# Cached attention on one core: key and value pages released and reloaded in runs of four, in place of whole batches

## The chip, the cores and the metric

The kernel runs on one core of one Trainium2 chip. The metric is device time in microseconds of one launch, lower is better. TensorE, VectorE (DVE), ScalarE (ACT), GpSimd (POOL) and SyncE (SP) each run a program of their own and meet through semaphores; SP and POOL also issue the DMAs.

## The reference, cut to what matters

One inference step of a two-layer decoder, for a prompt of 256 tokens and for 8 sample batches of 8 tokens each. The sample batches attend to a past of 2048 rows that lies in a paged cache: 16 pages of 128 rows for each batch, at places that a page table gives. Everything is float32.

```
past = cache_kv[page_table, :, c].reshape(Bd, past_len, N_KV, HEAD_DIM)   # c: 0,1 compressed  2 keys  3 values
...
idx = top_k(score, 16)                   # selected blocks of 64 rows, from the compressed branch's weights
s   = q . k * scale - slopes * dist      # over the selected blocks of the past
p   = masked_softmax(s)
o_s = p . v
o_w = window_dense(q, qpos, kw, vw)      # the same over the last 512 rows, from state_kv_win
o   = gates[0] * o_c + gates[1] * o_s + gates[2] * o_w
```

The change touches only how the key pages (c = 2), the value pages (c = 3) and the window rows of the sample batches come into SBUF, and when their buffers are free again. The feed-forward parts, the convolution, the prompt's attention and the compressed branch are as they were.

## The kernel before

The kernel is written engine by engine: `sp_program`, `pool_program`, `pe_program`, `act_program` and `dve_program`, each in its own order, with counting semaphores between them. The cached attention comes after the prompt's attention and ahead of the output projection `o`. It goes over the 8 batches b, NB = 8, with NPAGE = 16 pages each.

**Buffers.** There is one key buffer `kpg` and one value buffer `vpg`, 16 pages of 128 KB each (128 rows by 256 numbers). The window rows of a batch (keys and values, 1 MB) go into one of the two slots of `W`, slot u = b mod 2. `KTb` and `KTw` hold the transposed keys of one batch, `S` its scores, `PT` its transposed probabilities.

**SP (`load_keys`).** For each batch: `load_pages` waits (L318) until the key buffer is free (K_used, once for each batch), then issues 16 page DMAs (L322), each behind a register load of the page's number (L320); then it waits until the window slot is free (win_used) and issues the window DMA (L455). After the last batch's keys SP loads the last batch's values into the key buffer as well, and then goes on to the weights of `o` (L470).

**POOL.** For batches 0 to 6 the same `load_pages` fills the value buffer, once V_used has risen for a whole batch.

**TensorE (`batch_scores`, `batch_values`).** The order is scores(0), then scores(b+1) and values(b) for b from 0 to 6, then values(7). scores(b) turns the probabilities of batch b-1 (L881) between the other steps, waits for all 16 key pages (K_loaded), turns the keys in 8 groups of four 128x128 transposes (`turn_keys`, L901; four page groups of the first 128 columns, then four of the other 128), turns the window's keys in two more groups, and multiplies the queries with the turned keys in chunks of 512 (L895). K_used rises with the first transpose of the window's groups. The groups go through two PSUM banks, which ACT (L1291) and DVE (L1791) copy out in turn. values(b) waits for all 16 value pages (V_loaded), multiplies the probabilities with three short blocks, with the four window blocks (win_used rises with the last of them, which frees the slot for batch b+2), and with the 16 pages (all L942). V_used rises with the first transpose of the result (L957).

**ACT and DVE** work the masked softmax of batch b while TensorE works values(b-1). DVE also places the queries and chooses the blocks.

Of the kernel before, what the change touches and what calls it, by code (L numbers as in the profile page):

```python
# [14 lines left out]
P = 128  # L15
# [3 lines left out]
NB = 8  # L19
# [12 lines left out]
NPAGE = 16  # L32
PAST = NPAGE * PAGE
NPOOL = 160
# [23 lines left out]
S_SEL, S_NEW, S_WIN, S_WNEW, S_CMP = 0, PAST, PAST + TS, PAST + TS + WIN, PAST + 2 * TS + WIN  # L58
S_COLS = S_CMP + P
CREDIT = 2  # L60


def host_constants():
# [94 lines left out]
def program(nc, ins, outs, where):  # L158
    with ExitStack() as ctx:
# [9 lines left out]
        def sem(name):  # L169
            return ctx.enter_context(nc.semaphore(name))  # L170
# [30 lines left out]
        ptrow = sb("ptrow", 1, P, dt=I32)  # L201
# [63 lines left out]
        kpg, vpg = pages  # L265
# [6 lines left out]
        KTb = area(SF, 0, 2, PAST)  # L272
# [26 lines left out]
        slab_loaded = [sem("slab_loaded0"), sem("slab_loaded1")]  # L299
        gathered = [sem("gathered0"), sem("gathered1")]  # L300
        half_used = [sem("half_used0"), sem("half_used1")]
        K_loaded, V_loaded, K_used, V_used = map(sem, ("K_loaded", "V_loaded", "K_used", "V_used"))
        V_last_loaded = sem("V_last_loaded")
        win_loaded = [sem("win_loaded0"), sem("win_loaded1")]
        win_used = [sem("win_used0"), sem("win_used1")]

# [5 lines left out]

        cache = ins["cache_kv"]

        def load_pages(eng, b, c, page, used, count, loaded):

            eng.wait_ge(used, count)
            eng.sem_inc(m["passed"], 1)  # L318
            for k in range(NPAGE):
                n = eng.value_load(ptrow[0:1, bass.ds(b * NPAGE + k, 1)], min_val=0, max_val=NPOOL - 1)  # L320
                src = cache[bass.ds(n, 1), :, c, :, :].rearrange("a t g d -> t (a g d)")
                eng.dma_start(page[:, k, :], src).then_inc(loaded, 16)  # L322


        def sp_program(sp):
# [123 lines left out]
            def load_keys(i, off):  # L449

                b, u = i * 2 + off, off % 2
                load_pages(sp, b, 2, kpg, K_used, b + 1, K_loaded)
                sp.wait_ge(win_used[u], i + (off // 2 + 1))
                sp.sem_inc(m["passed"], 1)
                sp.dma_start(W[:, u, :], ins["state_kv_win"].rearrange("b (p r) c g d -> b p (r c g d)", r=WR)  # L455
                             [bass.ds(b, 1)].rearrange("a p c -> p (a c)")).then_inc(win_loaded[u], 16)

            load_keys(0, 0)
            with sp.Fori(0, NB // 2 - 1) as i:
# [1 line left out]
                    load_keys(i, u + 1)  # L461
            load_keys(NB // 2 - 1, 1)

            load_pages(sp, NB - 1, 3, kpg, K_used, NB + 1, V_last_loaded)
            wo = ins["w_o"][0].rearrange("(q g z d) n -> q g d z n", q=2, g=2, z=NZ)

            def out_proj(i, u):
# [11 lines left out]
        def pool_program(pool):  # L479
            pool.memset(eps[:, :], EPS).then_inc(m["pool_step"], 1)  # L480
            pool.memset(ones[:, :], 1.0).then_inc(m["pool_step"], 1)
            pool.memset(HF[:, 0:1], 0.0).then_inc(m["pool_step"], 1)
            pool.wait_ge(m["idx_ready"], 1)
            pool.wait_ge(m["evac_done"], OUTS_DOWN00 + CREDIT)
            pairs = cache.rearrange("n t (h c) g d -> (n t h) (c g d)", h=2)
            with pool.Fori(0, NB) as b:
                for u in range(2):
                    pool.wait_ge(half_used[u], b + 1)

                    pool.tensor_copy(cslot[:, 8 * u:8 * u + 8], cidx[:, bass.ds(b * CS + 8 * u, 8)]) \  # L490
                        .then_inc(m["slot_ready"], 1)
                    pool.wait_ge(m["slot_ready"], b * 2 + (u + 1))
                    pool.sem_inc(m["passed"], 1)
                    for s in range(8):
                        pool.indirect_dma_start(  # L495
                            out=STG[u][:, s, :], out_offset=None, in_=pairs,
                            in_offset=bass.IndirectOffsetOnAxis(ap=cslot[:, 8 * u + s:8 * u + s + 1], axis=0)) \
                            .then_inc(gathered[u], 16)

            pool.dma_start(outs[5].rearrange("b t c g d -> b (t c g d)")[:, 0:(WIN - NQ) * 512],  # L500
                           ins["state_kv_win"].rearrange("b t c g d -> b (t c g d)")[:, NQ * 512:]) \
                .then_inc(m["stored"], 16)
            pool.dma_start(outs[7][0, :, 0:HIST - NQ, :], ins["state_conv"][0, :, NQ:, :]).then_inc(m["stored"], 16)

            pool.wait_ge(m["conv_rows"], 4)
            pool.dma_start(outs[6][0, 0], convP).then_inc(m["conv_stored"], 16)
            for b in range(NB):
                pool.dma_start(outs[7][0, b, HIST - NQ:, :], convS[b * NQ:b * NQ + NQ, :]) \
                    .then_inc(m["conv_stored"], 16)

            pool.wait_ge(m["evac_done"], OUTS_KV + CREDIT)
            flat = [outs[2][0].rearrange("(t p) c g d -> p t (c g d)", p=P),
                    outs[4][0].rearrange("(t p) c g d -> p t (c g d)", p=P)]
            for o, (c, n), done in zip(flat, ((0, 4), (4, 2)), (m["kv_stored"], m["stored"])):
                pool.dma_start(o, rows[:, :, c:c + n, :].rearrange("p t c d -> p t (c d)")).then_inc(done, 16)
            pool.dma_start(outs[3].rearrange("b t c g d -> (b t) (c g d)"),
                           rowsS[:, 0:4, :].rearrange("p c d -> p (c d)")).then_inc(m["stored"], 16)
            for b in range(NB):
                pool.dma_start(outs[5].rearrange("b t c g d -> b t (c g d)")[b, WIN - NQ:, :],
                               rowsS[b * NQ:b * NQ + NQ, 4:6, :].rearrange("p c d -> p (c d)")) \  # L520
                    .then_inc(m["stored"], 16)

            pool.wait_ge(m["ptrow_loaded"], 16 * 9)
            pool.wait_ge(m["kv_out"], 2 * (NB + 1))
            with pool.Fori(0, NB - 1) as b:
                load_pages(pool, b, 3, vpg, V_used, b + 1, V_loaded)
            pool.wait_ge(m["y_out"], 6)
            pool.dma_start(outs[0][0].rearrange("(t p) d -> p t d", p=P), yout[:, 0:2, :]).then_inc(m["stored"], 16)
            pool.dma_start(outs[1].rearrange("b t d -> (b t) d"), yout[0:TS, 2, :]).then_inc(m["stored"], 16)
            pool.wait_ge(m["kv_stored"], 16)  # L530
            pool.wait_ge(m["conv_stored"], 16 * (NB + 1))
            pool.wait_ge(m["stored"], 16 * (2 + 2 + NB + 2))


        def pe_program(pe):
            seen = Seen()
            outs_ = [0]
            for s, n in ((m["slab_used"], CREDIT), (K_used, 1), (V_used, 1), (win_used[0], 1), (win_used[1], 1)):
                pe.sem_inc(s, n)

            def product(out, w, x, start, stop):
# [342 lines left out]
            def batch_scores(i, off, before):  # L884
# [13 lines left out]
                def turn_keys(r, tiles):  # L898
                    pe.wait_ge((m["kt_out0"], m["kt_out1"])[r % 2], b * 5 + (r // 2 + 1))
                    for c, t in enumerate(tiles):  # L900
                        mm = pe.transpose(PS[r % 2][:, c * P:c * P + P], t, ident)  # L901
                        if r == 8 and c == 0:
                            mm.then_inc(K_used, 1)
                    mm.then_inc(m["kt_turned"], 1)

# [7 lines left out]
                chunk(0, [(0, TS, lambda q: kT[:, 0, q, SEQ:]), (TS, TS, lambda q: kT[:, 1, q, SEQ:]),  # L913
                          (2 * TS, P, lambda q: kcT[:, bass.ds(b, 1), q, :].rearrange("p a n -> p (a n)"))])
                turn_before(2)
                pe.wait_ge(K_loaded, b * 256 + 256)
                for r in range(8):
                    turn_keys(r, [kpg[:, 4 * (r % 4) + c, (r // 4) * P:(r // 4) * P + P] for c in range(4)])
                    if r in (1, 3, 5):
                        turn_before(3 + r // 2)  # L920
                pe.wait_ge(win_loaded[u], i * 16 + (off // 2 * 16 + 16))
# [13 lines left out]
                    chunk(c + 1, [(0, 512, lambda q: KTb[:, q, c * 512:c * 512 + 512])])  # L935
                chunk(5, [(0, WIN, lambda q: KTw[:, q, :])])

            def batch_values(i, off, page=vpg, loaded=None):
                b, u = i * 2 + off, off % 2

                def value(c, n, v, first=False, last=False):
                    return pe.matmul(PS[7][:, 0:256], PT[0:n, c * P:c * P + P], v, start=first, stop=last)  # L942

                pe.wait_ge(*(loaded or (V_loaded, b * 256 + 256)))
                pe.wait_ge(m["o_copied"], b + 1)
                pe.wait_ge(m["pt_out"], b * 6 + (6 + CREDIT))
                value(0, TS, rowsS[:, 3, :], first=True)
# [3 lines left out]
                    mm = value(3 + c, P, wst[u][:, c, 256:512])  # L951
                mm.then_inc(win_used[u], 1)
                for k in range(NPAGE):
                    mm = value(7 + k, P, page[:, k, :], last=k == NPAGE - 1)
                mm.then_inc(m["o_ready"], 1)
                pe.wait_ge(m["o_copied"], b + 2)
                pe.transpose(PS[4][:, 256:384], osb[:, 0:P], ident).then_inc(V_used, 1)  # L957
# [9 lines left out]
            for g in range(6):  # L967
                turn_probs(NB - 1, g)
            pe.wait_ge(m["o_out"], 2 * (NB - 1))
            batch_values(NB // 2 - 1, 1, kpg, (V_last_loaded, 16 * NPAGE))  # L970
            pe.wait_ge(m["o_out"], 2 * NB)
            slabs("o", pair, first=rows_in())
            ffn("11")
# [10 lines left out]
        def act_program(act):  # L984
# [301 lines left out]
            def batch_scores(b, last):  # L1286

                def keys(r):
                    act.wait_ge(m["kt_turned"], b * 10 + (r + 1))
                    dst = KTb[:, r // 4, (r % 4) * 512:(r % 4) * 512 + 512] if r < 8 else KTw[:, r - 8, :]  # L1290
                    act.activation(dst, PS[r % 2][:, :], ACT.Copy).then_inc(m["kt_out0"], 1)  # L1291

                def before(g):
# [46 lines left out]
        def dve_program(dve):  # L1340
# [428 lines left out]
            def batch_scores(b):  # L1769
# [17 lines left out]

                def keys(r):
                    dve.wait_ge(m["kt_turned"], b * 10 + (r + 1))
                    dst = KTb[:, r // 4, (r % 4) * 512:(r % 4) * 512 + 512] if r < 8 else KTw[:, r - 8, :]  # L1790
                    dve.tensor_copy(dst, PS[r % 2][:, :]).then_inc(m["kt_out1"], 1)  # L1791

                def normalise(src, col):
# [149 lines left out]
```

## Time and profile before

| | us |
|---|---|
| median of 3 runs | 2042.19 |
| lowest and highest | 2037.63, 2045.8 |
| span of the profiled execution, first to last instruction | 1995.8 |
| what lies around the span, median less span | 46.4 |
| cached attention, from the first scores to the last value product | about 1412 to 1700 |

No time of its own is shown for the profiled execution, so its span is set against the median. Times in rows are microseconds from the start of the span unless marked ns. An engine named with a q (SPq, POOLq) is its sequencer: register, branch, semaphore and DMA-issuing instructions, which are not counted as busy. A float32 matmul shows as two instructions on TensorE.

### The profile page before, as it was taken

The numbers are of one execution on the slowest core, as the hardware profiler recorded it, in microseconds if no ns is written. First come the engines' busy times: TensorE is split into PE (matmuls) and PEld (weight loads), VectorE is DVE, ScalarE is ACT, GpSimd is POOL, SyncE is SP. The second block draws the span as 40 slices with busy tenths as digits, with TensorE's granted clock in tenths as the row PEclk, the third lists the DMA queues.
The fourth block names the chain that finished last, engine by engine and source line by source line (L and its number), as shares of the span: only waits on it lengthen the run. The fifth ranks groups of instructions, "written<-read, shape, count | busy, mean of one in ns | idle before, by whom it ended". The sixth has DMA issues, their size and how long they took to land.

```text
span 1995.8 us, 34060 instructions
## 1 busy us (share of the span) xinstructions
PE 1860.9 (93%) x11395; PEld 1705.2 (85%) x11395; DVE 1203.2 (60%) x2309; ACT 758.6 (38%) x1244; POOL 208.0 (10%) x288
## 2 busy tenths in 40 slices
PE   7999998999997999999999999989698888899996
PEld 6999998888885899999999999778466666899995
DVE  6665564897976766554666553355455554666654
ACT  4332343565655333332333333567132323333321
POOL 0000030444540000000100000100011321000000
PEclk9999997999997999999999998577699999899998
DMA  5556582443444455454555464300134443455552
GB/s 157 149 148 168 148 245 72 118 135 107 135 155 191 127 147 148 142 152 143 150 147 147 137 158 96 127 1 0 64 119 155 148 167 116 117 153 151 139 145 70
DMA packets 367902, 264.18 MB, mean 132 GB/s; under 512 B 30863, under 2 KB 350850, under 8 KB 366544
## 3 DMA queue, kind: packets, MB, share of 16 engines
q1 hardware_dynamic: 350496, 202.47, 36.2%
q0 software_dynamic: 17344, 60.89, 9.5%
q8 instruction: 38, 0.62, 0.1%
q14 instruction: 24, 0.20, 0.0%
HBM read 259.65 MB, written 12.64 MB: 136 GB/s over the span
## 4 chain that ended last, share of the span: by engine, by line
PE 83%; DVE 5%; issue 4%; ACT 3%; DMA 1%; POOL 1%; POOLq 1%; SPq 1%; DVEq 0%; ACTq 0%
PE PSA L544 21%; PE PSA L546 21%; PE PSA L545 21%; PE PSA L942 4%; PE PSA L655 3%; PE PSA L895 2%; PE PSA L839 1%; POOL G_f L322 1%; POOLq L320 1%; PE PSA L817 1%; DVE S_f32r L1357 1%; PE PSA L795 1%; PE PSA L819 1%; DMA G_f<-in_cache_kv 1%; PE PSA L901 1%
## 5 line engine op out<-in xcount | busy, mean ns | idle before, releaser
L544 PE MATMUL PSA<-H_f32r,S_f32r 128*128 128x320 f32 (+1 forms) x1984 | 656.5, 331 | 24.0 <-DVE H_f32r L1493 23.6
L546 PE MATMUL PSA<-H_f32r,S_f32r 128*128 128x320 f32 (+1 forms) x1984 | 641.8, 323 | 0.0
L545 PE MATMUL PSA<-H_f32r,S_f32r 128*128 128x320 f32 x1728 | 539.2, 312 | 0.0
L1357 DVE TENSOR_TENSOR S_f32r<-W,S_f32r 128x2048 fp32r<-128x2048 f32 (+1 forms) x178 | 365.0, 2051 | 118.5 <-ACT S_f32r L998 111.0
L544 PEld LDWEIGHTS PSA<-H_f32r,S_f32r 128*128 128x128 f32 x1984 | 379.0, 191 | 35.6 <-issue 23.9
L998 ACT ACTIVATE S_f32r<-W 128x2048 fp32r<-128x2048 f32 (+1 forms) x178 | 305.2, 1715 | 271.1 <-PE PSA L546 263.8
L546 PEld LDWEIGHTS PSA<-H_f32r,S_f32r 128*128 128x128 f32 x1984 | 378.2, 191 | 11.6
L545 PEld LDWEIGHTS PSA<-H_f32r,S_f32r 128*128 128x128 f32 x1728 | 329.4, 191 | 0.4
L545 PE MATMUL PSA<-G_f32r,S_f32r 128*128 128x320 f32 (+1 forms) x960 | 320.2, 334 | 0.0
L544 PE MATMUL PSA<-G_f32r,S_f32r 128*128 128x320 f32 x704 | 217.6, 309 | 1.2 <-DVE S_f32r L1357 1.2
L546 PE MATMUL PSA<-G_f32r,S_f32r 128*128 128x320 f32 x704 | 217.5, 309 | 0.0
L1031 ACT ACTIVATE tmp<-tmp 128x320 f32<-128x320 f32 x96 | 45.3, 472 | 441.3 <-DVE tmp L1427 441.3
L545 PEld LDWEIGHTS PSA<-G_f32r,S_f32r 128*128 128x128 f32 x960 | 182.3, 190 | 5.9
L1427 DVE TENSOR_TENSOR tmp<-PSA,stat 128x320 f32<-128x320 f32 x96 | 47.2, 491 | 179.9 <-PE PSA L546 179.0
L1600 DVE SCALAR_TENSOR_TENSOR H_f<-G_f,wdw,H_f 128x256 f32<-128x256 f32 x480 | 152.0, 378 | 0.0
L495 POOL DMA_INDIRECT G_f<-in_cache_kv,cslot x128 | 128.3, 1002 | 48.9 <-issue 35.8
L544 PEld LDWEIGHTS PSA<-G_f32r,S_f32r 128*128 128x128 f32 x704 | 132.1, 188 | 1.5 <-issue 1.5
L546 PEld LDWEIGHTS PSA<-G_f32r,S_f32r 128*128 128x128 f32 x704 | 132.1, 188 | 0.0
L322 POOL DMA_DIRECT2D G_f<-in_cache_kv x112 | 60.3, 538 | 644.0 <-issue 644.0
L1090 ACT ACTIVATE H_f32r<-PSA 128x512 fp32r<-128x512 f32 x128 | 76.7, 599 | 115.5 <-PE PSA L655 114.7
L1590 DVE TENSOR_TENSOR G_f32r<-PSA,H_f32r 128x512 fp32r<-128x512 f32 x128 | 88.1, 689 | 50.9 <-ACT H_f32r L1090 50.8
L655 PEld LDWEIGHTS PSA<-const,W 128*128 128x128 f32 (+1 forms) x576 | 74.6, 154 | 26.0 <-issue 4.9
(252 smaller groups left out, 2235.5 us busy)
## 6 DMA issues: line engine op xcount, KB each, us to landing
W<-in_w_ff_in SPq DMA_DIRECT2D x176, 512.0 KB, 4.8
W<-in_w_ff_out SPq DMA_DIRECT2D x64, 704.0 KB, 4.6
G_f<-in_cache_kv SPq DMA_DIRECT2D x144, 128.0 KB, 2.3
G_f<-in_cache_kv POOLq DMA_DIRECT2D x112, 128.0 KB, 2.7
W<-in_w_pw SPq DMA_DIRECT2D x16, 512.0 KB, 5.1
W<-in_state_kv_win SPq DMA_DIRECT2D x8, 1024.0 KB, 4.8
out_win_sample<-in_state_kv_win POOLq DMA_DIRECT2D x1, 8064.0 KB, 9.9
W<-in_w_kv SPq DMA_DIRECT2D x6, 1024.0 KB, 5.0
```

Of the source, the lines that this page charges most:

```text
L322: eng.dma_start(page[:, k, :], src).then_inc(loaded, 16)
L495: pool.indirect_dma_start(out=STG[u][:, s, :], out_offset=None, in_=pairs, in_offset=bass.IndirectOffsetOnAxis(ap=cslot[:, 8 * u + s:8 * u ...
L544: pe.matmul(out, w[0], x[0], start=start, stop=False)
L545: pe.matmul(out, w[0], x[1], start=False, stop=False)
L546: return pe.matmul(out, w[1], x[0], start=False, stop=stop)
L655: tr = pe.transpose(PS[5 + c][:, g * n:g * n + n], RL[0:n, c, g * P:g * P + P], ident[0:n, 0:n])
L942: return pe.matmul(PS[7][:, 0:256], PT[0:n, c * P:c * P + P], v, start=first, stop=last)
L998: act.activation(flat_slab[u][HI][:, 0:ph.cols], flat_slab[u][RAW][:, 0:ph.cols], ACT.Copy) \
L1090: act.activation(self.RT[:, j % 2, c, 0:4 * n], PS[5 + c][:, 0:4 * n], ACT.Copy) \
L1357: dve.tensor_tensor(lo, raw, hi, ALU.subtract).then_inc(m["lo_ready"], 1)
L1590: dve.tensor_tensor(RTs[1][:, j % 2, c, 0:4 * P], PS[5 + c][:, 0:4 * P], RTs[0][:, j % 2, c, 0:4 * P], ALU.subtract).then_inc(m["rt_ready" ...
L1600: dve.scalar_tensor_tensor(o, x(b * TAPS_AT_ONCE + (a + 1)), wdw[:, bass.ds(b * (TAPS_AT_ONCE * KT) + (a * KT + KT + k), 1)], o, ALU.mult, ...
```

## The change

The 16 pages of a batch are cut into four runs of four pages (RUN = 4, RUNS = 4). Each run has its own loaded semaphore, K_loaded[r] and V_loaded[r]. K_used and V_used rise four times a batch. `load_pages` waits for one release before each run. `turn_keys` takes the groups in page order, so that both column halves of a run are turned one after the other, and K_used rises with the first transpose of groups 2, 4, 6 and 8; ACT and DVE write `KTb` to match. values(b) waits before each run of pages, and V_used rises after the fourth, eighth and twelfth page and at L957. In `load_keys` the window's wait and DMA stand ahead of the pages. POOL loads the values of all 8 batches; SP no longer loads the last one's.

```
-        def load_pages(eng, b, c, page, used, count, loaded):
-            eng.wait_ge(used, count)
-            eng.sem_inc(m["passed"], 1)
-            for k in range(NPAGE):
-                n = eng.value_load(ptrow[0:1, bass.ds(b * NPAGE + k, 1)], min_val=0, max_val=NPOOL - 1)
-                src = cache[bass.ds(n, 1), :, c, :, :].rearrange("a t g d -> t (a g d)")
-                eng.dma_start(page[:, k, :], src).then_inc(loaded, 16)
+        def load_pages(eng, b, c, page, used, loaded):
+            for r in range(RUNS):
+                eng.wait_ge(used, b * RUNS + (r + 1))
+                eng.sem_inc(m["passed"], 1)
+                for k in range(r * RUN, r * RUN + RUN):
+                    n = eng.value_load(ptrow[0:1, bass.ds(b * NPAGE + k, 1)], min_val=0, max_val=NPOOL - 1)
+                    src = cache[bass.ds(n, 1), :, c, :, :].rearrange("a t g d -> t (a g d)")
+                    eng.dma_start(page[:, k, :], src).then_inc(loaded[r], 16)
...
             def load_keys(i, off):
                 b, u = i * 2 + off, off % 2
-                load_pages(sp, b, 2, kpg, K_used, b + 1, K_loaded)
                 sp.wait_ge(win_used[u], i + (off // 2 + 1))
                 sp.sem_inc(m["passed"], 1)
                 sp.dma_start(W[:, u, :], ...).then_inc(win_loaded[u], 16)
+                load_pages(sp, b, 2, kpg, K_used, K_loaded)
...
-            load_pages(sp, NB - 1, 3, kpg, K_used, NB + 1, V_last_loaded)
...
-            with pool.Fori(0, NB - 1) as b:
-                load_pages(pool, b, 3, vpg, V_used, b + 1, V_loaded)
+            with pool.Fori(0, NB) as b:
+                load_pages(pool, b, 3, vpg, V_used, V_loaded)
...
-                        if r == 8 and c == 0:
+                        if r in (2, 4, 6, 8) and c == 0:
                             mm.then_inc(K_used, 1)
...
-                pe.wait_ge(K_loaded, b * 256 + 256)
                 for r in range(8):
-                    turn_keys(r, [kpg[:, 4 * (r % 4) + c, (r // 4) * P:(r // 4) * P + P] for c in range(4)])
+                    if r % 2 == 0:
+                        pe.wait_ge(K_loaded[r // 2], b * (16 * RUN) + 16 * RUN)
+                    turn_keys(r, [kpg[:, RUN * (r // 2) + c, (r % 2) * P:(r % 2) * P + P] for c in range(RUN)])
...
-                pe.wait_ge(*(loaded or (V_loaded, b * 256 + 256)))
...
                 for k in range(NPAGE):
-                    mm = value(7 + k, P, page[:, k, :], last=k == NPAGE - 1)
+                    if k % RUN == 0:
+                        pe.wait_ge(V_loaded[k // RUN], b * (16 * RUN) + 16 * RUN)
+                    mm = value(7 + k, P, vpg[:, k, :], last=k == NPAGE - 1)
+                    if k % RUN == RUN - 1 and k < NPAGE - 1:
+                        mm.then_inc(V_used, 1)
...
-                    dst = KTb[:, r // 4, (r % 4) * 512:(r % 4) * 512 + 512] if r < 8 else KTw[:, r - 8, :]
+                    dst = KTb[:, r % 2, (r // 2) * 512:(r // 2) * 512 + 512] if r < 8 else KTw[:, r - 8, :]
```

The last pair of lines stands in `act_program` and in `dve_program` alike.

## Rows read from the trace of the kernel before

**Rows 1.** The page's head: span, and busy time of the matrix engine.

```profile
span 1995.8 us, 34060 instructions
PE 1860.9 (93%) x11395; PEld 1705.2 (85%) x11395; DVE 1203.2 (60%) x2309; ACT 758.6 (38%) x1244; POOL 208.0 (10%) x288
```

**Rows 2.** Waits, 1400 to 1710 us: us in total, times, longest.

```profile
PE PSA L942 <- DMA G_f<-in_cache_kv: 12.1, 5, 3.7
```

**Rows 3.** Chain of waits in order of time: start us, us, what; values(0), (3), (6), (7).

```profile
1464.88 10.34 PE PSA L942 x46
...
1509.54 0.34 PE PSA L957
...
1565.07 3.27 DMA G_f<-in_cache_kv
...
1568.46 10.40 PE PSA L942 x46
...
1672.05 12.09 PE PSA L942 x46
...
1689.39 10.38 PE PSA L942 x46
```

**Rows 4.** Timeline of PE, 1600 to 1645 us: start, us, line, operation [idle before].

```profile
1602.34 1.12 PE L942 MATMUL PSA<-rowsS,G_f 64*128 64x256 f32 x4 [1.90 <-DMA G_f<-in_cache_kv]
...
1605.66 7.07 PE L942 MATMUL PSA<-G_f 128*128 128x256 f32 x32
...
1615.61 1.10 PE L895 MATMUL PSA<-kT,G_f 128*128 128x64 f32 x8 [1.21 <-DVE G_f L1774]
...
1617.48 1.04 PE L901 MATMUL PSA<-const,G_f 128*128 128x128 f32 x8
...
1618.83 1.14 PE L901 MATMUL PSA<-const,G_f 128*128 128x128 f32 x8
...
1621.67 1.17 PE L901 MATMUL PSA<-const,G_f 128*128 128x128 f32 x8
...
1627.21 7.11 PE L895 MATMUL PSA<-S_f,G_f 128*128 128x512 f32 x16
1636.59 1.12 PE L942 MATMUL PSA<-rowsS,G_f 64*128 64x256 f32 x4 [2.27 <-DMA G_f<-in_cache_kv]
```

**Rows 5.** Timeline of SP's queue: keys of batch 6, a window, keys of batch 7.

```profile
1590.38 18.20 SPq L322 DMA_DIRECT2D G_f<-in_cache_kv  x16
1608.92 0.33 SPq L455 DMA_DIRECT2D W<-in_state_kv_win  x1
...
1624.18 17.34 SPq L322 DMA_DIRECT2D G_f<-in_cache_kv  x16
```

**Rows 6.** Timeline of POOL: the first two value pages of batch 2.

```profile
1511.26 0.54 POOL L322 DMA_DIRECT2D G_f<-in_cache_kv  x1 [14.93 <-issue]
1512.49 0.54 POOL L322 DMA_DIRECT2D G_f<-in_cache_kv  x1 [0.69 <-issue]
```

**Rows 7.** Line L318, the wait for a free buffer: ns min/median/max.

```profile
L318 SPq EVENT_SEMAPHORE  x9: 17/17/28, 1269.3 to 1657.6; - x9
```

**Rows 8.** DMA issues, KB each, median us to landing: 1488 to 1497, then 1454 to 1474.

```profile
G_f<-in_cache_kv SPq DMA_DIRECT2D x8, 128.0 KB, 2.8
...
G_f<-in_cache_kv SPq DMA_DIRECT2D x16, 128.0 KB, 2.2
W<-in_state_kv_win SPq DMA_DIRECT2D x1, 1024.0 KB, 4.8
```

**Rows 9.** Windows: us, busy PE, PEld, DVE, ACT, POOL, granted clock, DMA share, GB/s.

```profile
1478.00:1482.00 4.00, 3.86 (x21) 3.87 (x22) 0.84 (x5) 0.60 (x1) 1.61 (x3) 0.61 0.27 98
...
1568.00:1602.00 34.00, 29.55 (x147) 21.07 (x147) 18.31 (x43) 9.58 (x21) 8.60 (x16) 1.00 0.45 153
```

**Rows 10.** Timeline of PE, 1464 to 1500 us, columns as in rows 4.

```profile
1478.14 1.32 PE L895 MATMUL PSA<-kT,G_f 128*128 128x64 f32 x8 [1.25 <-DVE G_f L1774]
...
1482.97 1.17 PE L901 MATMUL PSA<-const,G_f 128*128 128x128 f32 x8
```

More of the change, by code:

```diff
@@ L60 @@
 CREDIT = 2
+RUN = 4
+RUNS = NPAGE // RUN
 def host_constants():
@@ L301, in program @@
         half_used = [sem("half_used0"), sem("half_used1")]
-        K_loaded, V_loaded, K_used, V_used = map(sem, ("K_loaded", "V_loaded", "K_used", "V_used"))
-        V_last_loaded = sem("V_last_loaded")
+        K_used, V_used = sem("K_used"), sem("V_used")
+        K_loaded = [sem(f"K_loaded{r}") for r in range(RUNS)]
+        V_loaded = [sem(f"V_loaded{r}") for r in range(RUNS)]
         win_loaded = [sem("win_loaded0"), sem("win_loaded1")]
@@ L537, in pe_program @@
             outs_ = [0]
-            for s, n in ((m["slab_used"], CREDIT), (K_used, 1), (V_used, 1), (win_used[0], 1), (win_used[1], 1)):
+            for s, n in ((m["slab_used"], CREDIT), (K_used, RUNS), (V_used, RUNS), (win_used[0], 1), (win_used[1], 1)):
                 pe.sem_inc(s, n)
@@ L936, in batch_scores, with batch_values @@
                 chunk(5, [(0, WIN, lambda q: KTw[:, q, :])])
-            def batch_values(i, off, page=vpg, loaded=None):
+            def batch_values(i, off):
                 b, u = i * 2 + off, off % 2
@@ L969, in pe_program @@
             pe.wait_ge(m["o_out"], 2 * (NB - 1))
-            batch_values(NB // 2 - 1, 1, kpg, (V_last_loaded, 16 * NPAGE))
+            batch_values(NB // 2 - 1, 1)
             pe.wait_ge(m["o_out"], 2 * NB)
@@ L1789, in keys @@
                     dve.wait_ge(m["kt_turned"], b * 10 + (r + 1))
-                    dst = KTb[:, r // 4, (r % 4) * 512:(r % 4) * 512 + 512] if r < 8 else KTw[:, r - 8, :]
+                    dst = KTb[:, r % 2, (r // 2) * 512:(r // 2) * 512 + 512] if r < 8 else KTw[:, r - 8, :]
                     dve.tensor_copy(dst, PS[r % 2][:, :]).then_inc(m["kt_out1"], 1)
```

## The prediction

> **What bounds the kernel now.** The page comes first: TensorE is busy for 93% of a span of 1995.8 us [rows 1], but that is an average over stages with different limits, and the diff touches one of them, the cached attention of the eight sample batches. So the waits of that stretch, 1400 to 1710 us, come next: its value matmuls (L942) stood 12.1 us in five waits on page transfers [rows 2]. The chain of waits confirms it for the end: a transfer of 3.27 us is over at 1568.3, and the value matmuls of batch 3 start at 1568.46 [rows 3].
>
> TensorE's order decides everything below: scores(0), scores(1), values(0), scores(2), values(1), ..., scores(7), values(6), values(7). I measure one turn from the start of values(b-2), called 0, to the start of values(b-1); scores(b) lies between. TensorE's timeline gives a turn at full clock, values(4) to values(5), 1602.34 to 1636.59 [rows 4]: window matmuls over at +3.32 (1605.66, where the page matmuls begin); the first eight key transposes at +15.14, the next eight at +16.49, then about +17.9 (halfway) and +19.33 (1621.67); last score matmul over at 1627.21 + 7.11 = 1634.32, +31.98; then 2.27 us idle on value pages. So TensorE alone needs some 32.1 us a turn, and the wait for values makes it 34.25. From values(0) to values(6), six turns, it was 1672.05 - 1464.88 = 207.2 us [rows 3].
>
> Keys are not late in this profile, and SP's timeline says why [rows 5]: the 16 pages of batch 6 are issued from 1590.38 for 18.20 us, as soon as scores(5) has turned batch 5's keys, and the window DMA follows at 1608.92. The last page is there some 6 us before scores(6) turns the first, at 1617.48.
>
> **Removed: the wait for whole batches of values.** V_used now rises after each four value pages and no longer at L957 alone, and TensorE waits run by run. POOL needs 1.23 us a page (1511.26 to 1512.49) and starts 1.4 us after a release (L957 was over at 1509.88) [rows 3, 6]. The 16 page matmuls take 7.07 us, 0.44 each [rows 4]: the first release comes at 3.3 + 4 x 0.44 = +5.1, the last page is issued at 5.1 + 1.4 + 15 x 1.23 + 0.3 for three run heads = +25.3, and lands near +28.2. The next turn wants it no earlier than 32.1 + 3.3 + 12 x 0.44 = +40.7. The 12.1 us go, if nothing else becomes late.
>
> **Moved: the window load, to the front of `load_keys`.** This decides. Window b goes into the slot that values(b-2) reads, and SP must see win_used before it loads it. Before, 16 page issues stood ahead of that wait; now the wait stands ahead of them. Queued behind it on SP are all four key runs of the batch, and TensorE's key transposes wait for those. The four K_used releases come during scores(b-1), all before values(b-2) starts, so from batch 2 on they are long given when SP reaches them: the early release of keys buys nothing, and keys start later than before. Batches 0 and 1 have free window slots; window 1 merely loads during the prompt's attention, where nobody waits for it.
>
> Key supply in a turn: win_used at +3.3; window DMA 0.4 later (between the last page's end, 1608.58, and the window DMA lay 0.34) and 0.33 long, over at +4.0 [rows 5]. First page about 0.95 later (18.20 us for 16 is 1.19 each, 0.85 without the 0.34 of an issue, and 0.1 for the new wait and count), +5.0; last page 17.9 later, and 0.1 for each of three further run heads, +23.2. A wait event took 17 ns [rows 7], so the heads could also cost next to nothing, 0.3 us less a turn. Landing: 2.2 us when SP loads alone, 2.8 while POOL loads too [rows 8]; here they overlap, and I take 2.7, and 0.1 to reach TensorE: +26.0. The window's own 1 MB lands 4.8 us after its issue, +8.5 [rows 8]; it delays the first pages, not the sixteenth, which is set by issue.
>
> What TensorE wants: run 0 at +15.1, lands +11.4; run 1 at +16.5, lands +16.2; run 2 at +17.9, lands +21.1, 3.2 us late; run 3 lands at +26.0, when run 2's transposes (1.4) have been over for 3.5 us. From run 3's first transpose to the end of the scores it is 1634.32 - 1621.67 = 12.65, and 0.1: the turn becomes **38.8 us**, a loop that returns to itself (values, window slot, 16 issues, landing, scores, values). The value pages, at +28.2, are ahead of it. The key load of batch 7, outside the loop, took 17.34 us for its 16 pages [rows 5], 0.9 less.
>
> Six turns: 5 x 38.8 + 37.9 = 231.9 against 207.2, **+24.7 us**. Bounds: landing 2.2 and free heads give 38.0 a turn, +20; landing 3.3, as in the chain [rows 3], gives 39.4, +28.
>
> **Clock.** TensorE is granted full speed over a turn whose pause is about 2 us (1.00 from 1568 to 1602), but 0.61 from 1478 to 1482, behind a pause of 1.25 us [rows 9, 10]. That drop cost 1482.97 - 1478.14 = 4.83 us against 1618.83 - 1615.61 = 3.22 for the same work, 1.6 us [rows 4, 10]; in values(6) it cost 12.09 - 10.40 = 1.7 [rows 3]. Each turn now has two pauses over 3 us within 8, the second right ahead of work on the path. Between none and two drops a turn I take 0.6 of one, 1.0 us: **+6.0**, with 0 and 6 x 3.2 = 19 as ends. The Trainium skill (TensorE: Matmul & The Clock Gate, section HAM oscillation) describes a loop with a transfer wait of several us in every step, in which every step starts at the lower clock. By that every turn would pay the 1.6 us, +9.6, and the sum would be 3.6 us more; the pauses inside these turns, 1 to 2.4 us, do not show whether it holds.
>
> **The end.** Batch 7's values came through SP into the key buffer and were there early: from values(6) to the last value matmul it took 1689.39 + 10.38 - 1672.05 = 27.7 us [rows 3]. Now POOL loads them behind batch 6's releases: last page lands +28.2, four more matmuls take 1.8, over at +30.1: **+2.4 us** (bounds 1 and 4, by the landing and a clock drop). SP is rid of 16 page issues, but its next wait is for values(6) all the same, so the output weights start at most a few us earlier, and they were hidden under the last values before.
>
> The new waits on TensorE come to eight a batch; at 17 ns for one that is met [rows 7] they are inside the rounding. The new order of the key turns keeps the count of transposes and copies. Nothing outside the cached attention changes.
>
> **Sum.** 24.7 + 6.0 + 2.4 = +33 us on the span of 1995.8. Some 46.4 us lie around that span in the median run of 2042.19, and I leave them: 2042 + 33 = **2075 us**. A difference under 0.5%, 10 us, could not be told from none here.
>
> **Rivals.** (1) *The split works and keys stay ahead*, the other side. For it: 12.1 us of value waits go [rows 2], and the keys have 6 us in hand now. Time: 2042 - 12.1 + 2.4 = 2032. It decides where run 3 lands, before +19.3: SP would have to get 16 pages out in 11.5 us. Against: 17.34 is the shortest shown [rows 5]. The Trainium skill (Perfetto Trace Analysis, section DMA Optimizations) holds that split transfers can start, and the whole end, sooner where DMA engines are idle. That rule speaks for this rival; here the transfers keep their size, and no run shows such a split. Chance 0.05. (2) *Keys late, but by little*: 1.13 us a page in every batch, as in the 17.34, landing 2.2, free heads and no clock drop give 37.1 a turn, +15, and with the end 2059. Chance 0.10. (3) *The clock stays down through the scores after each pause*: the 7.11 us of score matmuls alone would double [rows 4], six times, 2042 + 27 + 43 = 2112. Against: behind that drop the eight transposes at 1482.97 took 1.17 us, as at full clock [rows 4, 10]. Chance 0.05. (4) *Keys late as worked out*: 0.80.
>
> **Range and chances.** The likeliest gives 2075. Its lower ends give 2042 + 20 + 0 + 1 = 2063, its upper ends 2042 + 28 + 19 + 4 = 2093 if they all came together; I take 2062 to 2088. That leaves out (1), (3) and most of (2), 2 in 10. Slower by over 0.5% holds (2), (3) and (4), 0.95; (1) lies at the bound, 0.03 faster and 0.02 within.
>
> **What would show it.** In the changed kernel SP issues each window before its pages, and from batch 2 on only after values(b-2) has begun; TensorE idles at the key transposes on page transfers, some 3 us twice a batch, and no longer at its value matmuls except in the last batch; values start 38 to 40 us apart; the granted clock dips in most turns. The prediction is wrong if values start 32 to 34 us apart, if key transposes wait for nothing, or if key pages are issued nearer than 1.1 us.

## The result, and the profile after

The changed kernel is slower: 2081.65 us median of 4 runs (2073.97 to 2085.62) against 2040.8 for the kernel before in the same series (2037.63 to 2045.8). The ratio is 1.0245, interval 1.0203 to 1.0288; the two medians by themselves stand at 1.020. The forecast was 2075, with 2062 to 2088. The median lies inside, but the ratio applied to 2040.8 gives 2091, just above the upper end. Runs of one kernel differ by tens of microseconds for a reason outside the change (below), so the stages of the profiles say more than the total. Here and below, ratios leave out executions more than 1.5% above the fastest of their kernel, medians and ranges keep them; one of those, in the experiment with one run ahead, took 3862.85 us at a mean granted clock of 0.479.

The page of the changed kernel begins:

```profile
span 2083.5 us, 34168 instructions
PE 1893.8 (91%) x11395; PEld 1725.4 (83%) x11395; DVE 1204.1 (58%) x2309; ACT 760.0 (36%) x1244; POOL 219.1 (11%) x304
```

The spans differ by 87.7 us [rows 1], about twice the difference of the times. Cut at the starts of the value matmuls (batch 0 and batch 6), at the first transpose of the last result and at the end:

| us | before | after | difference |
|---|---|---|---|
| up to values(0) | 1464.8 | 1509.6 | +44.7 |
| values(0) to values(6), six turns | 207.2 | 242.2 | +35.0 |
| values(6) to the last result's transpose | 28.2 | 37.4 | +9.2 |
| from there to the end | 295.6 | 294.3 | -1.3 |

The first line is not the change's. It follows POOL's indirect gathers for the compressed branch, a stage the diff does not touch. Here is that line's group in the kernel before (count, ns, first and last start in us):

```profile
L495 POOL DMA_INDIRECT G_f<-in_cache_kv,cslot x128: 942/948/1907, 268.7 to 584.3; - x128
```

and in the changed kernel, where the last gather starts 45 us later:

```profile
L498 POOL DMA_INDIRECT G_f<-in_cache_kv,cslot x128: 942/950/1905, 268.0 to 629.5; - x128
```

So the first profile had caught a quick execution: in the other nine profiles of this document the last gather starts at 630 to 654 us. What lies around a span is about 2 us (2085.62 against 2083.5 in the profiled run here), not the 46.4 that the prediction took; it added its sum to a measured time, so this did not move the forecast. The other three lines, +42.9 us, are the change's own, to within the 3 us by which the same stage of the kernel before differed between two profiles (next section).

Waits of the changed kernel, 1445 to 1800 us (us in total, times, longest), answer to [rows 2]: the value matmuls' five waits have become one, at the end, and the key transposes (L904), which waited for no transfer before, now do.

```profile
PE PSA L904 <- DMA G_f<-in_cache_kv: 29.2, 11, 3.8
...
PE PSA L946 <- DMA G_f<-in_cache_kv: 8.6, 1, 8.6
```

SP's own waits in that stretch name the cause. L457 is the wait for the window slot, ahead of the keys, released by a value matmul in six batches:

```profile
SPq L457 <- PE PSA L946: 132.1, 6, 31.0
```

One turn of TensorE, values(0) to values(1), to be read against [rows 4]:

```profile
1509.56 1.13 PE L946 MATMUL PSA<-rowsS,G_f 64*128 64x256 f32 x4
...
1512.88 7.07 PE L946 MATMUL PSA<-G_f 128*128 128x256 f32 x32
...
1525.79 1.64 PE L904 MATMUL PSA<-const,G_f 128*128 128x128 f32 x8
...
1530.65 1.09 PE L904 MATMUL PSA<-const,G_f 128*128 128x128 f32 x8 [1.34 <-DMA G_f<-in_cache_kv]
...
1535.96 1.09 PE L904 MATMUL PSA<-const,G_f 128*128 128x128 f32 x8 [3.78 <-DMA G_f<-in_cache_kv]
1537.30 1.97 PE L904 MATMUL PSA<-const,W 128*128 128x128 f32 x8 [0.25 <-ACT S_f L1298]
...
1540.24 3.78 PE L898 MATMUL PSA<-S_f,G_f 128*128 128x512 f32 x4 [0.54 <-DVE S_f L1798]
...
1544.09 7.11 PE L898 MATMUL PSA<-S_f,G_f 128*128 128x512 f32 x16
1551.13 1.13 PE L946 MATMUL PSA<-rowsS,G_f 64*128 64x256 f32 x4
```

SP's queue in the same turn, against [rows 5]: window first, 3.7 us into the turn, then sixteen pages.

```profile
1513.29 0.33 SPq L458 DMA_DIRECT2D W<-in_state_kv_win  x1
1514.65 18.91 SPq L326 DMA_DIRECT2D G_f<-in_cache_kv  x16
```

The last page has landed, and the fourth run's transposes start, 26.4 us into the turn. In the kernel before that group started at +19.33 [rows 4]. Behind it the window keys take 1.97 us and the first score chunk 3.78 us, where the undisturbed turn of the next section has 1.27 and 1.98. The windows of that stretch give the granted clock (third number from the end):

```profile
1532.00:1536.00 4.00, 0.22 (x3) 0.04 (x1) 0.47 (x1) 0.60 (x1) 1.62 (x3) 1.00 0.61 196
1536.00:1540.00 4.00, 3.44 (x18) 2.91 (x18) 1.39 (x3) 1.46 (x3) 0.00 (x0) 0.66 0.09 33
1540.00:1545.00 5.00, 4.76 (x8) 2.26 (x9) 0.98 (x4) 0.01 (x1) 0.00 (x0) 0.59 0.00 0
1545.00:1551.00 6.00, 6.00 (x15) 2.47 (x13) 3.06 (x10) 0.00 (x0) 0.00 (x0) 1.00 0.00 0
```

In this turn it is at 1.00 in the wait itself, lower once the work has resumed, and back at 1.00 from 1545 on, for the rest of the scores.

### The profile page after: what moved, and what is told of

It is laid out like the page before. It is cut to its first block, busy times and chain, and to the rows that moved or that the text cites. A ratio compares the mean times of both kernels' runs of the same rounds, so it can differ in the third digit from the quotient of the medians.

```text
span 2083.5 us, 34168 instructions
## 1 busy us (share of the span) xinstructions
PE 1893.8 (91%) x11395; PEld 1725.4 (83%) x11395; DVE 1204.1 (58%) x2309; ACT 760.0 (36%) x1244; POOL 219.1 (11%) x304
## 4 chain that ended last, share of the span: by engine, by line
PE 77%; DVE 6%; issue 5%; SPq 5%; ACT 3%; DMA 2%; another core or an unknown queue 1%; DVEq 1%; POOLq 0%; POOL 0%; ACTq 0%
PE PSA L547 20%; PE PSA L548 19%; PE PSA L549 19%; PE PSA L898 4%; PE PSA L658 3%; SPq L324 2%; SPq L326 2%; PE PSA L946 2%; PE PSA L904 1%; PE PSA L842 1%; DVE H_f L1607 1%; DMA G_f<-in_cache_kv 1%; PE PSA L820 1%; DVE S_f32r L1364 1%
## 5 line engine op out<-in xcount | busy, mean ns | idle before, releaser
L547 PE MATMUL PSA<-H_f32r,S_f32r 128*128 128x320 f32 (+1 forms) x1984 | 659.8, 333 | 34.0 <-DVE H_f32r L1500 24.4
L549 PEld LDWEIGHTS PSA<-H_f32r,S_f32r 128*128 128x128 f32 x1984 | 380.1, 192 | 12.6
L548 PE MATMUL PSA<-G_f32r,S_f32r 128*128 128x320 f32 (+1 forms) x960 | 324.4, 338 | 0.0
L326 POOL DMA_DIRECT2D G_f<-in_cache_kv x128 | 71.0, 555 | 699.8 <-issue 695.7
```

The costliest lines, as they stand in the source:

```text
L326: eng.dma_start(page[:, k, :], src).then_inc(loaded[r], 16)
L547: pe.matmul(out, w[0], x[0], start=start, stop=False)
L548: pe.matmul(out, w[0], x[1], start=False, stop=False)
L549: return pe.matmul(out, w[1], x[0], start=False, stop=stop)
```

## The experiments

All stages below are read from the experiment's profile at the same marks. "Turns" is values(0) to values(6), six turns; "end" is values(6) to the first transpose of the last result. The experiments ran in two later series, in which the kernel before took 2053.16 and 2054.84 us in the median, so a time is read by its ratio to the kernel before, and a single run by its stages alone.

**The kernel before, again.** No edit.

> The kernel before, once more, to see where its profiled execution of 1995.8 us and its timed runs of about 2040 us part. Theory: outside the change, in the stage of page gathers for the compressed branch (268 to 612 us in the profile of before, 268 to 657 in that of after), so the span is about 2038 us, that stage is some 45 us longer than in the first profile, and values(0) to values(6) take 207 us again. Rival: the cached attention itself varies by tens of us, and values(0) to values(6) come out far from 207.

Turns 210.6, end 28.2, span 2065.5; its time was 2067.17. The last gather started later still:

```profile
L495 POOL DMA_INDIRECT G_f<-in_cache_kv,cslot x128: 945/949/2876, 269.0 to 649.7; - x128
```

The place was right, the size not: 65 us later than in the first profile, and not 45. In this series the kernel before ran from 2043.75 to 2079.11. The six turns moved by 3 us. Why the gathers vary was not tried.

**Window behind the keys.**

```
             def load_keys(i, off):
                 b, u = i * 2 + off, off % 2
+                load_pages(sp, b, 2, kpg, K_used, K_loaded)
                 sp.wait_ge(win_used[u], i + (off // 2 + 1))
...
-                load_pages(sp, b, 2, kpg, K_used, K_loaded)
```

> The changed kernel with only the window's wait and DMA put back behind the sixteen page issues; runs, semaphores, key order and value loading stay changed. Theory (the window wait ahead of the keys is the cost): no wait of TensorE on pages in the turns, 32 to 33 us a turn, values(0) to values(6) about 193 to 198 us in place of 242; the end after values(6) stays long, about 37 us; time about 2081 - 46 = 2035 us. Rival (cutting into runs costs: more waits, two transposed halves at a time, run semaphores): turns stay near 41 us and the time near 2080.

Turns 193.0, end 37.9; 2045.67 us median, ratio to the kernel before 0.9964 (0.9925 to 1.0003). Five of the six turns are 31.7 to 31.9 us, and not one key transpose waits for a page. One such turn on TensorE, the undisturbed turn meant above:

```profile
1585.83 1.13 PE L946 MATMUL PSA<-rowsS,G_f 64*128 64x256 f32 x4
...
1605.16 1.17 PE L904 MATMUL PSA<-const,G_f 128*128 128x128 f32 x8
1606.50 1.27 PE L904 MATMUL PSA<-const,W 128*128 128x128 f32 x8 [0.17 <-ACT S_f L1298]
...
1608.74 1.98 PE L898 MATMUL PSA<-S_f,G_f 128*128 128x512 f32 x4 [0.75 <-DVE S_f L1798]
...
1610.70 7.11 PE L898 MATMUL PSA<-S_f,G_f 128*128 128x512 f32 x16
1617.74 0.48 PE L946 MATMUL PSA<-rowsS,G_f 64*128 64x256 f32 x1
```

SP there begins a batch's keys 14.2 us ahead of the turn (1571.63 against 1585.83), not 5.1 us into it, and the window follows them:

```profile
1571.63 18.70 SPq L326 DMA_DIRECT2D G_f<-in_cache_kv  x16
1590.67 0.33 SPq L459 DMA_DIRECT2D W<-in_state_kv_win  x1
```

The 49 us between these turns and the changed kernel's come from the order of two steps in one queue. Runs, semaphores and key order cost nothing that shows: with them the turns are 14 us shorter than before. The long end, 9.7 us more than before, takes most of that back, which is why the time is hardly below the kernel before.

**One run ahead of the window.** Run 0, window, runs 1 to 3.

```
+                load_pages(sp, b, 2, kpg, K_used, K_loaded, range(1))
                 sp.wait_ge(win_used[u], i + (off // 2 + 1))
...
-                load_pages(sp, b, 2, kpg, K_used, K_loaded)
+                load_pages(sp, b, 2, kpg, K_used, K_loaded, range(1, RUNS))
```

> The changed kernel with the window's wait and DMA between the first and the second key run: twelve page issues behind the wait and not sixteen. Theory (SP's issue time behind the wait sets the turn, 1.18 us a page): the last page is issued 4 x 1.18 = 4.7 us sooner in the turn, lands at about +21.6 against the +19.3 at which it is wanted; turns of about 34.5 us at full clock, up to 37 with a clock drop; time about 2045 us. Rival (the 1 MB window transfer and the value pages crowd the key pages): the last run lands as late as before, turns stay near 40 us, time near 2075.

Turns 203.9, 34.0 each; 2058.91 us, ratio 1.0048 (1.0006 to 1.0091). The fourth run is turned 21.2 us into the turn, 5.2 sooner than in the changed kernel, for four pages fewer behind the wait:

```profile
1545.20 1.13 PE L947 MATMUL PSA<-rowsS,G_f 64*128 64x256 f32 x4
...
1563.11 1.17 PE L905 MATMUL PSA<-const,G_f 128*128 128x128 f32 x8
1566.38 1.09 PE L905 MATMUL PSA<-const,G_f 128*128 128x128 f32 x8 [1.67 <-DMA G_f<-in_cache_kv]
...
1578.88 1.13 PE L947 MATMUL PSA<-rowsS,G_f 64*128 64x256 f32 x4
```

The expectation had 4.7. The turns gain 3 us on the kernel before, and the end, 37.6 us, loses 9. The window's megabyte and the value pages are issued as they were in the changed kernel, 3.7 and 6.6 us into the turn; the lateness follows the count of issues behind the wait. That fits the first theory and not crowding.

**Window by POOL.** The wait and the DMA leave SP and stand on POOL ahead of the value pages of the batch before.

```
-                sp.wait_ge(win_used[u], i + (off // 2 + 1))
-                sp.sem_inc(m["passed"], 1)
-                sp.dma_start(W[:, u, :], ...).then_inc(win_loaded[u], 16)
...
+                pool.wait_ge(win_used[u], i + (off // 2 + 1))
+                pool.sem_inc(m["passed"], 1)
+                pool.dma_start(W[:, u, :], ...).then_inc(win_loaded[u], 16)
...
+                for off in (2, 3):
+                    load_window(i, off)
+                    load_pages(pool, i * 2 + (off - 1), 3, vpg, V_used, V_loaded)
```

> The changed kernel with the window DMAs and their wait moved from SP to POOL, ahead of the value pages of the batch before; SP issues key pages alone. The window is loaded at the same point of the turn as in the changed kernel, only not ahead of the keys in SP's queue. Theory (what costs is the place of the wait in the queue of the keys): turns of 32 to 33 us, values(0) to values(6) about 193 us. Rival (loading the window at that point, just ahead of the pages, is what makes the keys late): turns near 40 us.

Turns 193.0, end 36.6; one run, 2041.43 us. POOL loads the window 4.2 us into a turn:

```profile
1582.38 0.54 POOL L531 DMA_DIRECT2D W<-in_state_kv_win  x1 [9.71 <-PE PSA L958]
1584.72 0.54 POOL L326 DMA_DIRECT2D G_f<-in_cache_kv  x1 [1.80 <-issue]
```

and the values start 31.9 us apart:

```profile
1578.14 1.13 PE L958 MATMUL PSA<-rowsS,G_f 64*128 64x256 f32 x4
1610.04 1.13 PE L958 MATMUL PSA<-rowsS,G_f 64*128 64x256 f32 x4
```

So loading the window at that point of the turn costs the keys nothing, as long as they do not stand behind its wait.

**Busy waits.** The identity is transposed into a free part of a bank, 4 and 12 times, ahead of two waits; nothing reads it.

```
                 for r in range(8):
+                    for _ in range({4: 4, 6: 12}.get(r, 0)):
+                        pe.transpose(PS[7][:, 256:384], ident, ident)
                     if r % 2 == 0:
```

> The changed kernel with 4 and 12 idle transposes of the identity into an unused part of a PSUM bank, ahead of the waits for the third and the fourth key run: TensorE is busy in most of the wait. Theory (part of each turn is lost to the clock that falls in the two waits): the granted clock stays at 1.00 behind the fourth run, from its first transpose to the values it takes 12.7 us in place of 13.9 to 15.2, turns of 39 to 39.5 us in place of 40.4 on average, time about 2074 us. Rival (the clock falls anyway, or the longer stretch has another cause): turns at 40.4 or more, time 2081 or more.

Turns 236.2, 39.4 each against 40.4, as expected; the time, 2096.54 with a ratio of 1.0214 (1.0144 to 1.0283), cannot be told from the changed kernel's. In three of the six turns, where the changed kernel has none, the whole stretch behind the fourth run, from its first transpose to the next values, is at full clock. Here it takes 12.6 us:

```profile
1560.54 1.09 PE L904 MATMUL PSA<-const,G_f 128*128 128x128 f32 x8 [0.92 <-DMA G_f<-in_cache_kv]
1561.88 1.19 PE L904 MATMUL PSA<-const,W 128*128 128x128 f32 x8 [0.25 <-ACT S_f L1300]
...
1564.13 1.98 PE L898 MATMUL PSA<-S_f,G_f 128*128 128x512 f32 x4 [0.84 <-DVE S_f L1800]
...
1573.13 1.13 PE L948 MATMUL PSA<-rowsS,G_f 64*128 64x256 f32 x4
```

In the next turn it is not: the same score chunk took 3.77 us, and the stretch, from 1599.51 to the values at 1614.64, 15.1. In the three turns at full clock TensorE had stood idle for 0.2 to 1.3 us ahead of the fourth run, in the other three for 2.0 to 2.3. So the clock is part of a turn's length, as the pair 12.6 and 15.1 shows, but these transposes do not hold it reliably, and the gain of 6 us over six turns is not a clean measure of it.

**Last values by SP.** As in the kernel before, in runs, into the key buffer.

```
+            load_pages(sp, NB, 3, kpg, K_used, K_loaded, NB - 1)   # ninth releases, page numbers of batch 7
...
-            with pool.Fori(0, NB) as b:
+            with pool.Fori(0, NB - 1) as b:
...
-            batch_values(NB // 2 - 1, 1)
+            batch_values(NB // 2 - 1, 1, kpg, K_loaded, NB)
```

> The changed kernel, with the values of batch 7 loaded as before: by SP, into the key buffer, ahead of the output weights, in four runs behind a ninth set of key releases; POOL loads batches 0 to 6. Theory (the end is long because POOL's last pages start late and share the DMA engines with the output weights, which SP now issues at once): from values(6) to the first transpose of the last result 28 us, as before, in place of 37.4; turns of about 40.4 us as in the changed kernel. Rival (the run waits inside the value matmuls make the end long): 37 us again.

End 26.5 us, 11 less than in the changed kernel; 2.8 of these 11 come back behind it (297.1 us to the end of the span, not 294.3). It is also 1.7 less than before, which is what the lower clock in values(6) had cost there. Turns 243.9. One run, 2086.37 us. The run waits inside the value matmuls are not what made the end long.

**Weights held.**

```
-            slabs("o", out_proj, first=[[(win_used[u], 1 + NB // 2)] for u in range(2)])
+            slabs("o", out_proj, first=[[(win_used[u], 1 + NB // 2), (V_loaded[RUNS - 1], NB * 16 * RUN)] for u in range(2)])
```

> The changed kernel, with SP held from the first two output weight slabs until batch 7's last value run has landed, so that those pages have the DMA engines to themselves. It tells the two parts of the long end apart. Theory (sharing makes about 7 of the 9 us): POOL's sixteen issues run at 1.23 us without the gap of 3 us, landing is about 2.8 us and not 8, and the last value matmul is over about 30 us after the start of values(6), as the prediction had it, in place of 37; the output projection then starts late instead, so the time need not fall. Rival (POOL's late start alone makes the end long): value matmuls over at 36 to 37 us again.

The value matmuls are over 34.2 us after the start of values(6) (1764.03 to 1798.23), between the two: 30 was expected, and the changed kernel has 37.0. A page lands 2.6 us after its issue again, but a gap of 3.2 us between POOL's first two issues stays, as in the changed kernel:

```profile
1770.62 0.54 POOL L326 DMA_DIRECT2D G_f<-in_cache_kv  x1 [20.46 <-issue]
1774.38 0.62 POOL L326 DMA_DIRECT2D G_f<-in_cache_kv  x1 [3.22 <-issue]
...
1791.99 0.54 POOL L326 DMA_DIRECT2D G_f<-in_cache_kv  x1 [0.68 <-issue]
```

and the last run of pages is multiplied at the lower clock, 3.68 us where the run before it took 1.99:

```profile
1789.53 1.99 PE L946 MATMUL PSA<-G_f 128*128 128x256 f32 x8 [2.93 <-DMA G_f<-in_cache_kv]
1794.55 3.68 PE L946 MATMUL PSA<-G_f 128*128 128x256 f32 x8 [3.03 <-DMA G_f<-in_cache_kv]
```

So sharing with the weights makes some 2.8 us of the end (37.0 less 34.2, one execution each), not the 7 that I held. The output projection starts late instead; the time was 2103.98 in one run.

**Both.** Window behind the keys and last values by SP.

> Window behind the keys and batch 7's values by SP into the key buffer, the rest as in the changed kernel. Theory: the two costs add, so values(0) to values(6) take 193 us, the end 28 us, together 221 against 235.4 in the profile of before and 279.6 in that of the changed kernel; about 14 us faster than before, 2027 where before has 2041, ratio 0.993. Rival (gains of the turns come back elsewhere): ratio 0.998 or more.

2034.52 us median of 12 runs, ratio 0.9922 (0.9887 to 0.9957), 0.993 expected: a little faster than the kernel before, and so than the changed kernel at 1.0245. Its profile is of the slowest of the twelve, 2058.47 us. There the end is 26.5 us; the turns are 197.8, three of 31.9 us and three of 33.3 to 35.1, so some 5 us of the gain expected there were missing in that execution. The three longer turns are longer ahead of the fourth run's transposes, where no page is waited for and the granted clock (third number from the end) is low; in the longest:

```profile
1619.00:1622.00 3.00, 3.00 (x16) 3.00 (x15) 1.37 (x5) 1.95 (x5) 1.41 (x3) 0.50 0.34 111
```

What let it fall there was not tried.

## Why the prediction was off: the place held, two terms were too small

**The step that decides**, the window's wait ahead of the keys, was right in direction, place and price. From batch 2 on SP waits for values(b-2) before it issues a key. Against the prediction's milestones in the turn shown: window DMA +3.7 (3.7 forecast), first page +5.1 (5.0), fourth run turned +26.4 (26.0), and +24.4 in the last turn (25.1). With the 12.6 us from there to the next values at full clock, five turns of 39.0 and one of 37.0 make 232, against the 231.9 of the forecast. Undoing the order took all of it away, and so did moving the wait to POOL; one run ahead took 5.2 us of lateness.

**The value waits** went, as forecast, in the turns. With the keys on time, 193 us against 207.2 is what that is worth: 14 us, where the prediction had 12.1. Most of the difference is a clock drop behind one of those waits: values(2) took 12.5 us in the kernel before, values at full clock 10.9.

**Clock: the first mis-sized term.** Six turns took 242.2 us, so 10 us lie above the 232 of the supply loop, where the prediction put 6.0. Its step "0.6 of one" drop a turn failed: every one of the six turns lost time to the lower clock behind the fourth run's wait. Against the undisturbed 12.6 us that stretch took 2.5 to 2.6 us longer in three turns and 0.7, 1.1 and 1.3 longer in the others. In the turn shown the 2.5 are the window keys and the first score chunk, 0.7 and 1.8 us longer. On average that is 1.8 a turn, near the 1.6 at which the prediction had priced a drop; so the count was wrong, and the price only on average right. The Trainium skill (TensorE: Matmul & The Clock Gate, section HAM oscillation) has every step of such a loop begin at the lower clock, which the prediction weighed at +9.6. The trace agrees that every turn pays; it differs in that in three of the six the eight transposes behind the wait are still at full clock (1.09 us), and only what follows is slower.

**The end: the second.** +9.2 us, not +2.4, and outside the prediction's own bounds of 1 and 4, where the clock's 10 us lay inside 0 and 19. The chain of the changed kernel's end, in order of time:

```profile
1758.37 0.32 POOL G_f L326
...
1762.12 0.33 POOL G_f L326
...
1774.66 8.23 DMA G_f<-in_cache_kv
1782.94 3.71 PE PSA L946 x8
1786.68 2.01 PE PSA L946 x8
```

POOL's first page was on time (+6.6), the second 3.8 us after it and not 1.2, so the last was issued at +28.0 and not +25.3. A page issued at 1774.66 was 8.23 us on its way, while SP was issuing loads of the output weights, four to a slab:

```profile
1755.26 45.02 SPq L473 DMA_DIRECT2D W<-in_w_o  x16
```

And eight of the last sixteen matmuls ran at the lower clock, 3.71 us in place of 2.0. The last value matmul was over at +37.0, 6.9 later than forecast. An estimate of the parts, from single executions: 2.8 us for the sharing, from the run with the weights held; 2.5 for the gap, 3.8 less 1.23; 1.7 to 1.9 for the clock. They make 7.0 to 7.2, about the 6.9.

The gap goes with the count of POOL's issues and not with the weights or the last batch. In all five profiles in which POOL loads the values of eight batches and no windows, it falls on the second page of batch 7, the 114th DMA that POOL issues for the cached attention. With the windows on POOL, the 114th is a page of batch 6, and there it is again:

```profile
1694.52 0.54 POOL L326 DMA_DIRECT2D G_f<-in_cache_kv  x1 [2.82 <-issue]
```

Where POOL issues 112, as in the kernel before, there is no such gap, so its rows could not show it. What makes it is not known.

The prediction named SP's freed time and the weights, but as something that was hidden anyway, and did not ask what they collide with. The Trainium skill (DMA: Bandwidth & Descriptors, section Issuing engines are not separate DMA queues) says that DMAs of all issuing engines run on the same 16 engines and interleave; the 8.23 us beside the weights and 2.6 without them agree.

**Sum.** Forecast 24.7 + 6.0 + 2.4 = 33; found 25 + 10 + 9.2 - 1.3 = 43. The medians differ by 41 and the ratio says 50; between these the runs do not decide. The rivals: keys that stay ahead (2032) fell, and are what the experiment with the window behind the keys comes to (its ratio of 0.9964 makes 2035 of the prediction's 2042); keys late by little fell, since the fourth run came at +26.4 and not some 2 us earlier; a clock that stays down through all the scores fell, since the last 7.11 us of scores run at full clock.

## What to carry to other kernels

In this kernel everything that stood behind a wait in SP's program took on the release time of that wait. Before two steps of such a program are swapped, put both release times and the issue time behind them on one axis: here 16 issues, 18.9 us together, came to stand behind the later of two releases. And when a change frees an issuing engine, ask what it issues next, and whose transfers that meets.

## What the runs showed of the hardware that was not expected

- The stage of indirect gathers varies between executions of the same code: in the kernel before its last issue started at 584 us in one profile and at 650 in another. That is more than the change under study, and one profile beside the times of other runs can mislead by as much.
- A clock drop cost 1.6 us in the kernel before, among the first scores and transposes of a turn, and up to 2.6 in the changed kernel, over the window keys and the first score chunk. That long matmuls pay more than steps that wait for copies would fit, but was not tried.
- The 114th DMA that POOL issued for the cached attention came after a gap of 2.8 to 3.2 us in place of 0.7, in all six profiles in which POOL issued that many. The weights are not its cause; what is stays open.
